# Expert weights as plain fp32 on two column halves, from a ring of nine blocks

## The reference

```python
def expert_block(args):
    xblk, e = args
    hid = jax.nn.silu(xblk @ w_gate[e]) * (xblk @ w_up[e])    # 1024 -> 512
    return hid @ w_down[e]                                    # 512 -> 1024
...
yr = yb.reshape(n_rows, d) * row_gate[:, None]
return jax.ops.segment_sum(yr, row_tok, num_segments=n_tok)
```

## Time and profile before

| | us |
|---|---|
| median of 3 runs | 1799.54 |
| lowest, highest | 1798.51, 1801.36 |
| span of the profiled execution | 1797.7 |
| TensorE busy, of the span | 1749.8 (97%) |
| VectorE busy | 1315.6 (73%) |
| ScalarE busy | 1027.7 (57%) |
| GpSimd busy | 230.2 (13%) |
| moved by DMA | 494.99 MB, mean 275 GB/s |

### The profile page before, as it was taken

How to read it: one execution, slowest core, us unless ns; L and a number is a source line. 1 busy time by engine, 2 the same in 40 slices (tenths; PEclk the granted TensorE clock), 3 DMA queues, 4 the chain that set the end, 5 groups by cost and what they waited for, 6 DMA issues and landing times.

```text
span 1797.7 us, 21881 instructions
## 1 busy us (share of the span) xinstructions
PE 1749.8 (97%) x7712; PEld 1178.3 (66%) x7719; DVE 1315.6 (73%) x1370; ACT 1027.7 (57%) x1067; POOL 230.2 (13%) x136
## 2 busy tenths in 40 slices
PE   8999998999999999999999999999899999999997
PEld 6876786565555555657787777878566665555564
DVE  4999767888888888875443533456988888888887
ACT  4225636777777777763221222233777777777774
POOL 0030001122221222100000000000122122221220
PEclk9999999999999999999999999999999999999999
DMA  8521056999999999995212221213999999999995
GB/s 285 188 94 48 13 199 242 400 408 406 408 405 399 400 402 399 400 358 180 92 50 94 94 94 47 94 69 116 356 403 409 414 407 406 411 404 400 410 388 223
DMA packets 101507, 494.99 MB, mean 275 GB/s; under 512 B 14153, under 2 KB 26441, under 8 KB 52160
## 3 DMA queue, kind: packets, MB, share of 16 engines
q1 hardware_dynamic: 88192, 467.69, 66.3%
q0 software_dynamic: 10176, 16.24, 2.7%
q10 hardware_dynamic: 3072, 10.18, 1.6%
HBM read 484.66 MB, written 26.74 MB: 284 GB/s over the span
## 4 chain that ended last, share of the span: by engine, by line
PE 52%; DMA 26%; DVE 12%; ACT 6%; issue 2%; SPq 1%; DVEq 0%; ACTq 0%
DMA raw<-in_expert_w_gate 26%; PE psum L927 8%; PE psum L928 8%; PE psum L929 8%; DVE w_lo L736 6%; ACT w_hi L749 5%; PE psum L1076 4%; PE psum L1010 4%; PE psum L1007 3%; PE psum L1460 2%; DVE xs L1947 2%; PE psum L1086 1%; PE psum L1091 1%; PE psum L1087 1%; PE psum L1028 1%
## 5 line engine op out<-in xcount | busy, mean ns | idle before, releaser
L736 DVE TENSOR_TENSOR w_lo<-raw,w_hi 128x2048 fp32r<-128x2048 f32 x290 | 663.0, 2288 | 164.0 <-ACT w_hi L749 157.1
L749 ACT ACTIVATE w_hi<-raw 128x2048 fp32r<-128x2048 f32 x290 | 552.3, 1911 | 215.7 <-DMA raw<-in_expert_w_up 88.5
L1010 PE MATMUL psum<-w_lo,uT_hi 128*64 128x512 f32 x992 | 270.8, 395 | 8.5 <-DVE w_lo L736 6.1
L714 ACT ACTIVATE w_hi<-raw 128x2048 fp32r<-128x2048 f32 x46 | 88.1, 1914 | 329.7 <-PE psum L929 329.5
L722 DVE TENSOR_TENSOR w_lo<-raw,w_hi 128x2048 fp32r<-128x2048 f32 x46 | 105.4, 2291 | 200.1 <-ACT w_hi L714 200.1
L1007 PE MATMUL psum<-w_hi,uT_hi 128*128 128x512 f32 x868 | 247.2, 401 | 1.7 <-DVE uT_hi L2226 1.7
L2560 POOL DMA_INDIRECT y_dram<-y_e,index x60 | 120.2, 2003 | 775.0 <-DVE y_e L2261 761.8
L1010 PEld LDWEIGHTS psum<-w_lo,uT_hi 128*64 128x64 f32 x992 | 130.8, 135 | 101.1 <-DVE w_lo L736 23.1
L1007 PEld LDWEIGHTS psum<-w_hi,uT_hi 128*128 128x128 f32 x868 | 160.5, 191 | 41.4 <-DVE uT_hi L2226 2.3
L2555 POOL DMA_INDIRECT x_e<-xs_dram,index x64 | 93.7, 1464 | 656.8 <-DVE index L2221 620.8
L927 PE MATMUL psum<-w_hi,uT_hi 128*128 128x512 f32 x352 | 139.1, 395 | 2.4 <-DVE h L2437 1.4
(11 more groups left out here) (272 smaller groups left out, 2523.5 us busy)
## 6 DMA issues: line engine op xcount, KB each, us to landing
raw<-in_expert_w_gate SPq DMA_DIRECT2D x128, 1024.0 KB
raw<-in_expert_w_up SPq DMA_DIRECT2D x128, 1024.0 KB
raw<-in_expert_w_down SPq DMA_DIRECT2D x68, 1024.0 KB
xs<-in_expert_w_down SPq DMA_DIRECT2D x60, 1024.0 KB, 14.2
raw<-in_odd_w_in SPq DMA_DIRECT2D x8, 2048.0 KB
raw<-in_odd_w_in SPq DMA_DIRECT2D x8, 1024.0 KB
raw<-in_odd_w_out SPq DMA_DIRECT2D x4, 2048.0 KB
raw<-in_even_w_in SPq DMA_DIRECT2D x3, 2048.0 KB
```

The source lines that it names most:

```text
L736: nc.vector.tensor_tensor(part(w_lo[b]), src, part(w_hi[b]).bitcast(F32), ALU.subtract).then_inc(m.lo[b], 1)
L749: nc.scalar.activation(part(w_hi[b]), src, ACT.Copy).then_inc(m.hi[b], 1)
L1010: mm = nc.tensor.matmul(psum[0:FIRST, bank], xeT_hi[:, 8 * b + 4 * half + j, 0:FIRST], lo[:, j], start=False, stop=False)
```

## The change

Expert products are plain fp32, with no split. For 64 tokens the stationary matrix is 64 columns wide, and the product's columns are cut in two: the left half of the output goes to PSUM partitions 0 to 63, the right half to 64 to 127, with the same tokens and the other half of the weights' columns. hid is then 128 partitions by 256, and its transposition takes two products instead of four. The wide step (BIG) is step 16, with full-width fp32 products. fold_in, low_part, stack_tokens and moe_split are gone; VectorE alone copies the transposed tokens, ACT alone the transposed hid. The two y copies each take one half of the partitions.

The buffers that the splits no longer need, with uT and xs, make a ring of nine blocks of 2 MB. Block n of the stream (gate, up, down of expert e in this order, n = 3e + kind) is loaded when block n - 9 has been used by its product. The first nine have conditions of their own in the dense stages (ring_free). Down's blocks are laid out by another order of rows, in which a packet has 4 KB instead of 8 KB. At the end SP asks for rows of tiles 0 and 1, then for v0, then for the rows of tiles 2 and 3. The loops over steps are unrolled. The order of experts to steps (spill lists, EARLY) is fitted to this: a few VectorE instructions more per routing, and 32 small products instead of 16 for the gates of slots (L1134). The two halves of the on-chip rows are added by products over 64 partitions each. The pass for overfull experts (over_pass, not run with these inputs) is rewritten to match.

```diff
-BIG = STEPS - 3
-SENT = STEPS - 2
-ANY = slice(2, BY_ROWS)
+EARLY = 3
+BIG = 16
+SENT = BY_ROWS
+ANY = slice(EARLY, BY_ROWS)
+RING = 3 * EARLY
...
-        wd_dram = expert_w_down.rearrange("l e (p j) n -> l e p (j n)", j=HC)
+        wd_dram = expert_w_down.rearrange("l e (j p) n -> l e p j n", j=HC)
...
+        in_pair = [place(f"in_pair{b}", [P, BLOCK], at=pair_at[b]) for b in range(2)]
+        ring = [[raw[1], raw[2], free_a, raw[0], in_pair[1], free_b, in_pair[0], in_uT, xs],
+                [raw[2], raw[0], free_a, raw[1], in_uT, free_b, in_pair[0], in_pair[1], xs]]
...
         def split_hi(act, n, halves=(0, 1)):
...
             for half in halves:
-                if n == first_odd or (n, half) == (first_odd + 1, 0):
-                    act.wait_ge(main.down_psum, STEPS)
+                if n == first_odd:
+                    act.wait_ge(*((main.gate_psum, STEPS - 2) if half == 0 else (main.up_psum, STEPS)))
...
+            def ring_free(layer, n):
+
+                if n == RING - 1:
+                    sp.wait_ge(xs_stored, 16 * (layer + 1))
+                    full_bank("norm", 2 * layer + 1, TILES - 1, 1)
+                elif not layer:
+                    if n in (0, 1, 3):
+                        sp.wait_ge(lo_ok[1], first_odd - 2 + (0, 1, None, 2)[n])
+                    elif n in (2, 5):
+                        sp.wait_ge(pv_done, TILES * A_HEADS)
+                        sp.wait_ge(csum, 6)
+                    elif n == 6:
+                        sp.wait_ge(*half_used(first_odd - 1, 0))
+                    else:
+                        full_bank("out0", 1, TILES - 1)
+                elif n in (0, 1, 3):
+                    sp.wait_ge(lo_ok[1], n_dense - 2 + (0, 1, None, 2)[n])
+                elif n == 2:
+                    full_bank("inner", R_HEADS - 1, TILES - 1)
+                    full_bank("yT", R_HEADS - 1, TILES - 1)
+                elif n == 4:
+                    full_bank("rg", R_HEADS - 1, TILES - 1)
+                elif n == 5:
+                    full_bank("out1", R_HEADS - 2, 1, TILES - 1)
+                else:
+                    full_bank("out1", R_HEADS - 1, n - 6, TILES - 1)
...
+                for e in range(STEPS):
...
+                    for kind, src in enumerate((wg_dram, wu_dram, wd_dram)):
+                        n = 3 * e + kind
+                        if n < RING:
+                            ring_free(layer, n)
+                        else:
+                            sp.wait_ge((m.gate_psum, m.up_psum, m.down_psum)[kind], past + e - EARLY + 1)
+                        w = ring[layer][n % RING]
...
+                            sp.dma_start(dst, part_of).then_inc(ring_landed[n % RING][half], 16)
+                sp.wait_ge(placed, 2 * layer + 2)
+                sp.wait_ge(m.xT_psum, STEPS * (layer + 1))
+                sp.wait_ge(m.y_free, SENT * (layer + 1))
+                load_rows(lambda q: rows_in[q], (0, 1))
                 if not layer:
                     odd_fill(odd_blocks[0])
-                sp.wait_ge(xs_stored, 16 * (layer + 1))
-                sp.wait_ge(placed, 2 * layer + 2)
-                sp.wait_ge(main.xT_psum, STEPS * (layer + 1))
-                sp.wait_ge(main.y_free, STEPS * (layer + 1))
-                load_rows(lambda q: rows_in[q], (0, 1))
-                sp.wait_ge(main.down_psum, STEPS * (layer + 1) - 1)
+                sp.wait_ge(m.down_psum, STEPS * (layer + 1) - 1)
                 load_rows(lambda q: rows_in[q], (2, 3))
...
+            def half_width(x, w, bank, ready, done):
+
+                for j in range(KC):
+                    if j % 4 == 0:
+                        ready(j // 4)
+                    for c in range(2):
+                        mm = nc.tensor.matmul(psum[c * FIRST:(c + 1) * FIRST, bank, 0:HID // 2], x[:, j, 0:FIRST],
+                                              w[:, j, c * HID // 2:(c + 1) * HID // 2], start=(j == 0), stop=(j == KC - 1))
+                mm.then_inc(done, 1)
...
+                    for c in range(2):
+                        mm = nc.tensor.matmul(psum[c * FIRST:(c + 1) * FIRST, bank],
+                                              x[:, j % 2, (j // 2) * FIRST:(j // 2 + 1) * FIRST],
+                                              w[:, j, c * 512:(c + 1) * 512], start=(j == 0), stop=(j == HC - 1))
+                mm.then_inc(done, 1)
...
+                for e in range(STEPS):
+                    if e:
+                        turned(e - 1)
+                    product = full_width if e == BIG else half_width
+                    pe.wait_ge(m.xT_ok, past + e + 1)
+                    product(xeT[:, e % 2], weights(3 * e, KC), 2, ready_of(3 * e), m.gate_psum)
+                    product(xeT[:, e % 2], weights(3 * e + 1, KC), 3, ready_of(3 * e + 1), m.up_psum)
+                    if e < STEPS - 1:
+                        pe.wait_ge(m.gathered[(e + 1) % 2], 16 * times(layer, e + 1))
+                        transpose_tokens(m, x_e[:, (e + 1) % 2], max(rows_in_step(e + 1), TURN_ROWS))
+                    if e:
+                        down(e - 1)
+                turned(STEPS - 1)
+                down(STEPS - 1)
```

More of the change, by code:

```diff
@@ L604, in is_down, with chunks_of @@
-        def is_down(k):
-            return k == n_moe - 1 or k >= 2 and (k - 2) % 3 == 2
-        def fills(layer, k, half):
-            def up_to(last):
-                return sum(1 for i in range(k % 2, last + 1, 2) if half or not is_down(i))
-            return layer * up_to(n_moe - 1) + up_to(k)
-        def per_turn(half):
-            return 2 + half
-        TURNS = (STEPS - 8) // 2
+        def chunks_of(w, j):
+            return w[:, :].rearrange("p (j n) -> p j n", j=j)
         def rows_in_step(e):
-            return P if type(e) is int and e == BIG else FIRST
@@ L672, in trunk_kernel @@
         half_count, count = {}, 0
-        for n in dense:
+        for n in range(n_dense):
             if not (n >= first_odd and odd_blocks[n - first_odd][0] == "wo"):
@@ L835, in free_half @@
-                def free_half(n, half, turn):
-                    k = n - first
-                    if not is_down(k) or k == n_moe - 1 or k == down_no(BIG + 1):
-                        freed(n - SLOTS, half, turn)
-                    elif k == down_no(0):
-                        sp.wait_ge(xs_stored, 16 * (layer + 1))
-                        if not half:
-                            b, _, full = banks.at("norm", 2 * layer + 1, TILES - 1, 1)
-                            sp.wait_ge(bank_full[b], full)
-                    elif k == down_no(1):
-                        freed(first + up_no(0), half)
-                    else:
-                        freed(n - 2 * SLOTS, half, turn)
@@ L850, in load_half @@
-                def load_half(kind, s, e, turn, half):
-                    src, number = {"gate": (wg_dram, gate_no), "up": (wu_dram, up_no), "down": (wd_dram, down_no)}[kind]
-                    n = first + number(s)
-                    c = slice(half * HALF, (half + 1) * HALF)
-                    block_half = one(src, layer, e)[:, c]
-                    free_half(n, half, turn)
-                    sp.dma_start(raw[slot_of(n)][:, c], block_half).then_inc((front, landed)[half][slot_of(n)], 16)
@@ L859, in experts, with expert @@
-                expert_steps(sp, load_step)
-                for half in range(2):
-                    load_half("down", STEPS - 1, STEPS - 1, 0, half)
+                def expert(step):
+                    if step < EARLY or step >= BY_ROWS:
+                        return step
+                    if step < BIG:
+                        return step + ((step + EXPERTS - spilled[0]) >> 5)
+                    if step == BIG:
+                        return spilled[0]
+                    return step - ((spilled[0] + (EXPERTS - step)) >> 5)
@@ L1773, in moe @@
+                kept(STEPS - 1)
                 act.wait_ge(spill_ok, layer + 1)
@@ L2263, in keep_y @@
[L2263 to L2276 removed]
+                dve.wait_ge(m.y_free, free)
@@ L2431, in residual @@
             def residual(hd, half):
-                if hd == R_HEADS - 1 and half:
-                    moe_split(dve, 1, "gate", 0, 0, True, (0,))
                 for q in range(TILES):
```

860 lines of the change are left out of this document (269 added, 591 removed).

## The result

The changed kernel takes 1770.8 us (median of 4 runs) against 1800.2: a ratio of 0.9833, 95% interval 0.9817 to 0.985. The gain is 29.4 us; 55 were forecast. One of its four runs, at 1808.5, fell in a disturbed state of the chip and is left out of the ratio.

What follows compares the result with a forecast made beforehand. DMA was taken to bound the expert streams, with column halves running together. Gains of 24.0 us (layer 0) and 30.9 us (layer 1), 54.9 in all, gave 1744.5 us; range 1726 to 1800 us, 8 times in 10.

Steps and rivals of the forecast that it cites:

- the likeliest case: Whole kernel: DMA-bound with column halves running together, chance 0.74, own range 1726 to 1770 us.
- DMA or ring worse: Expert streams: dearer blocks or a ring not full in time, 1770 to 1797 us, chance 0.06.
- DMA gives less: Rival, expert streams: 5.6 us a block by dearer packets or waiting refills, 1776 us; within a band of chance 0.06.
- TensorE's step: Expert steps: 12 us if the two column halves run at once, 22.1 us if not.
- The rate of the weights: Mid-stream: 0.6% lost to down's 4 KB packets, giving 5.44 us a block in layer 0 and 5.39 in layer 1.
- 85 x 5.44: Layer 0's stream: 85 blocks following each other behind block 11's issue, 462.7 us in the sum.
- 85 x 5.39: Layer 1's stream: 85 blocks following each other, ending at 1739.4.
- The start of the stream: Behind the first product: block 11 goes out when down(0) is used, at about +20.5 us; DMA idles some 6 us.
- Layer 0's first product: Start of layer 0's experts: first product at about 279.0, 2.1 us later (between 0 and 4).
- The clock's fall: Rival, mid-stream: TensorE's clock drops to 1.2 GHz; about 2290 us if for good; chance 0.03.
- Tails: Behind the last weights: layer 1's first product at E + 23.4, gain taken as 24.0; layer 1's add_last at E + 9.5.
- Layer 1's first product: Start of layer 1's experts: 1.2 us later by its own chain (0.5 to 2.3).

Runs made afterwards that it cites:

- experiment 1: Changed kernel with each product's left column half done for all chunks before the right half, instead of alternating; 1946.4 us.
- Experiment 3: Runs on block cost: two_rows; ring_three; a ring of four from block thirty, with loads in order of use (1754.9 us); changed kernel with token rows reordered (1790.4 us).
- serial: The run of experiment 1: changed kernel with the column halves one after the other instead of alternating; 1946.4 us.
- two_rows: Changed kernel with gather and scatter moving 2 rows instead of 64 (or 128) from the third expert on; 1703.3 us.
- ring_three: Changed kernel, but from expert 10 on a block is asked for when the block three before it, not nine, has been used; 2209.3 us.
- tail_order: Changed kernel with the first split of layer 1's first dense block v0 moved behind the norm's Square and root of tile 0; 1767.4 us.
- kb8_down: Changed kernel with down's blocks laid out so that each packet has 8 KB again; 1762.8 us.
- experiment 2: Changed kernel with blocks 4 to 8 of each layer's ring asked for only when the first expert's tokens have been transposed; 1792.1 us.

## Why the prediction was right, and where it was off

The sign, the bound and the mechanism were right: DMA-bound with the halves together. The time is in the range of 1726 to 1800, but the gain was forecast at nearly twice what it is. 1770.8 is also just above the likeliest case's own range (to 1770), in the band "DMA or ring worse" that had a chance of 0.06, and of the rivals "DMA gives less" (5.6 us a block, 1776) comes nearest to what happened: 5.53 and 5.48. Two terms that were too high take 3.7 us off those that were too low; that much is luck. Point by point, on the clock of the profiled execution (1742.8 forecast, 1768.7 measured, 25.9 over):

- **TensorE's step**: 12 us forecast, 12.07 measured (293.89 to 305.96). The reading of the score products, row halves at once and so column halves too, was right; experiment 1 shows it. Its weight loads, 0.14 us each, show nowhere in it, though both halves share all rows. By the sentence of the Trainium skill (TensorE: Matmul & The Clock Gate, Part 3: Packing small matmuls) that a load overlaps running products only where the row group differs, they should have, and the trace disagrees. The prediction left out that the same part of the Trainium skill also lets a load go ahead when it targets the background weight buffer; whether that is what happens here, no run shows.
- **The rate of the weights**: 403 GB/s less 0.6% were forecast for layer 0, 397 to 403 came. Right for the median engine (5.44 and 5.40 us a block). The term that was too small is "85 x 5.44" and "85 x 5.39" (the first is 462.4; the 462.7 of the sum comes from the unrounded rate): it took the mean of the engines for the time at which blocks land. A block waits for the slowest, 84 x 0.086 and 84 x 0.080 = 7.2 and 6.7 us more. The earlier trace rows can't show this, as they are means; the landings in the trace of before could have. There, the loads of down into xs in layer 0, from the one asked for at 311.09 to the one at 732.46, 78 blocks later, land 5.50 us a block apart by their last arrivals and 5.41 by their median ones. Their drift stays at 8 us or less. Experiment 3 shows that without most of the tokens' traffic the lag grows by 0.034 and 0.059 us a block instead of 0.086 and 0.080, and that the row's position matters; where the rest comes from is open.
- **The start of the stream**: down(0) was used at +20.95 (20.5 forecast), but block 11, asked for with 12 and 13 behind it, landed 9.9 and 9.1 us later, where 5.4 had been taken: with the later use, +4.9 and +4.0. About half of that is not the company: block 9, the first behind a gap as well, with the next one asked for only 3.1 us later, took 7.6 us from its issue to its last arrival in both layers (288.96 to 296.53 in layer 0). So 2.2 us is what it costs over the pace of the stream, and 2.3 and 1.6 us come on top for block 11, with 12 and 13 asked for 1.3 and 2.4 us later; that this is their share of the engines is my reading, no run tests it. This and the drift come to 12.1 and 10.7 of the 12.0 and 11.8 us by which the streams were longer; in layer 1 the median block was 0.01 us dearer as well (5.40 for 5.39, 1.1 us).
- **Layer 0's first product**: 284.75 for 279.0, 5.75 over. 2.5 were lost before (the dense stage ended at 246.84 instead of 244.31), 1.5 are filler products at the lower clock, the rest is the gather, behind more weights than I had counted. A part belongs to this one execution: in serial, two_rows, ring_three and tail_order, which start with the same code, the dense stage ends at 245.4 to 245.5 and the first product comes at 282.7 to 283.1, and in kb8_down at 245.6 and 286.4. The clock's fall was a rival for mid-stream; there its mean stays at 0.98 to 1.00, and the short falls like that at 612.9 are covered by the wait for weights.
- **Tails** (E is the last landing of a layer's weights, 779.99 and 1742.78): E + 22.6 for the first product of layer 1, where the chain gave 23.4 and the sum took 1.2 more; add_last of layer 1 at E + 8.1 (9.5). The wait of ScalarE for v0 was forecast and is there, 4.01 us, and ends at E + 10.4 instead of E + 12.4. Together with the stretch between, 2.5 us under.
- **Layer 1's first product**: 1.2 later forecast by its own chain, none measured (32.60 us behind the end of the dense products, 32.56 before): 1.2 under.

Sum: 12.0 + 11.8 + 5.75 - 2.5 - 1.2 = 25.9.
The bounds of the own range had 1.5% of the rate for this; the loss by drift and by the late block 11 was 2.5% of each stream. That the gain is mostly the filled ring is shown by one run (experiment 2: 21 of 29).

## What to carry to other kernels

When a stream of loads is at a DMA share of 1, cost it by when loads land, not by the mean rate: look at the landings' first, median and last arrival. Load in the order in which the blocks are used, or the first one that waits for a late use holds all behind it. Count a first load behind a gap at its own time from issue to landing, not at the stream's pace. Half-wide fp32 products pay when the two halves are neighbours in the queue. Once an engine is freed, what decides is what was filled before its first product, and what stands in a queue ahead of the first small transfer.

## What the runs showed of the hardware

- Two products of 64 stationary columns on different column halves of the array start 7 ns apart in the single records (293.895 and 293.902) and run at once, 0.216 us per record of 256 fp32 columns, two records to a product; and so do the end of one half's row of products and the start of the other's, with no order written for it.
- The 16 arrivals of one load drift apart, to 16 to 19 us over some 70 blocks of 2 MB with a ring of nine, and then stay so. A ring of four blocks had 11 us and cost nothing in one run; the loads into xs of the kernel before, with its four slots, had 8.2 at most.
- Without most of the gathers and scatters (3.9% of the bytes) the weights' own packets got 2% (8 KB) and 5% (4 KB) shorter in 400 to 700, and a block of the median engine 6 to 7% cheaper.
- The position of the rows in a gather or scatter of 64 matters: another order of rows cost 1.1% of the kernel with the same bytes.
- The weights' packets of 4 KB took 171.6 ns in the mean of 400 to 700, those of 8 KB 321.4: 6.8% more per byte. Without the former, a block was 1.0 and 0.7% cheaper.
- The first block of 2 MB asked for behind a gap, with no other for 3.1 us, took 7.6 us to land; in the stream one lands every 5.5 us.
- TensorE's granted clock was 0.50 (1.2 GHz) behind the wait of 4.91 us, for the transposes, the fillers and the start of the first product (0.74 in the mean of 280 to 290), and 0.50 in 612.9 to 616.1 behind a wait of 2.70 us; in 605 to 612, with waits of 0.5 and 0.6 us before it, it was 1.00.
